# Holding x by features instead of by tokens through two transformer blocks, with each norm's root multiplied into the projections' results

## What is computed

```python
def rmsnorm(x, w):                       # norm_a, norm_c, final_norm; the second block's norms alike
    y = x * rsqrt(mean(x * x, axis=-1, keepdims=True) + EPS)
    return y * w
...
x = x + even_layer(rmsnorm(x, norm_a), w_in_a, ...)     # differential attention and a state-space scan
x = x + odd_layer(rmsnorm(x, norm_c), w_in_c, b_in_c, ...)   # sliding-window attention
x = rmsnorm(x, final_norm)
h = x + hybrid_mixer(rmsnorm(x, norm_mix), w_in, ...)   # stick breaking and two sparse attentions
h = h + memory_attention(h, mem, norm_mem_q, ...)
h = h + swiglu(rmsnorm(h, norm_ffn), w_ffn_in, w_ffn_out)   # (silu(a) * b) @ w_ffn_out, 2816 wide
return rmsnorm(h, norm_final)
```

## Time and profile before

| | us |
|---|---|
| median of 3 runs | 1584.45 (1584.28 to 1588.25) |
| the profiled execution, its own time | 1584.13 |
| its span | 1581.9 |
| PE busy in the span | 1534.0 (97%) |
| DVE, ACT, POOL busy | 820.4, 666.7, 260.6 |
| transfers | 150.20 MB, mean 95 GB/s |

### The profile page before, as it was taken

One profiled execution on the slowest core, in us unless ns is written; L12 is line 12 of the kernel. 1 busy time (PEld: TensorE's weight loads), 2 busy tenths in 40 slices (PEclk: granted clock), 3 DMA queues, 4 the chain that ended last, 5 costly groups with the idle time before them and its releaser, 6 DMA issues. The chain is left out here.

```text
span 1581.9 us, 20868 instructions
## 1 busy us (share of the span) xinstructions
PE 1534.0 (97%) x7886; PEld 1266.7 (80%) x7886; DVE 820.4 (52%) x1610; ACT 666.7 (42%) x1385; POOL 260.6 (16%) x166
## 2 busy tenths in 40 slices
PE   9999999999999999998999999899999999999998
PEld 7888878888787889877888777678866888888886
DVE  4322289858734566536634477847666333333224
ACT  4222366566424377524235554643245322232122
POOL 0000044265300012200012232313311000000000
PEclk9999999999999999999999999999999999999999
DMA  5226255311322431023521211213211222322322
GB/s 215 94 94 186 94 154 153 94 54 54 120 94 68 148 86 54 28 93 107 149 94 54 80 56 59 101 41 107 94 67 54 94 94 97 103 93 93 105 95 80
DMA packets 47458, 150.20 MB, mean 95 GB/s; under 512 B 6464, under 2 KB 6848, under 8 KB 47232
## 3 DMA queue, kind: packets, MB, share of 16 engines
q1 hardware_dynamic: 41664, 136.34, 26.8%
q10 hardware_dynamic: 5696, 12.55, 2.6%
HBM read 128.02 MB, written 2.10 MB: 82 GB/s over the span
## 5 line engine op out<-in xcount | busy, mean ns | idle before, releaser
L224 ACT ACTIVATE cut_hi<-raw 128x1024 fp32r<-128x1024 f32 x228 | 241.7, 1060 | 575.5 <-PE ps L241 571.2
L241 PE MATMUL ps<-h_hi,cut_hi 128*128 128x512 f32 (+1 forms) x1120 | 446.3, 399 | 5.5 <-DVE h_lo L449 2.8
L229 DVE TENSOR_TENSOR cut_lo<-raw,cut_hi 128x1024 fp32r<-128x1024 f32 x172 | 214.4, 1246 | 456.6 <-ACT cut_hi L224 454.9
L243 PE MATMUL ps<-h_hi,cut_lo 128*128 128x512 f32 (+1 forms) x1120 | 435.4, 389 | 0.0
L242 PE MATMUL ps<-h_lo,cut_hi 128*128 128x512 f32 (+1 forms) x1120 | 435.0, 388 | 0.0
L241 PEld LDWEIGHTS ps<-h_hi,cut_hi 128*128 128x128 f32 x1120 | 210.6, 188 | 56.2 <-issue 13.0
L243 PEld LDWEIGHTS ps<-h_hi,cut_lo 128*128 128x128 f32 x1120 | 210.4, 188 | 44.6
L242 PEld LDWEIGHTS ps<-h_lo,cut_hi 128*128 128x128 f32 x1120 | 210.9, 188 | 37.6
L229 POOL TENSOR_TENSOR cut_lo<-raw,cut_hi 128x1024 fp32r<-128x1024 f32 x56 | 135.4, 2418 | 467.4 <-ACT cut_hi L224 467.4
L241 PE MATMUL ps<-cut_hi,h_hi 128*128 128x512 f32 (+1 forms) x304 | 117.5, 387 | 3.3 <-DVE cut_lo L229 2.9
L243 PE MATMUL ps<-cut_hi,h_lo 128*128 128x512 f32 (+1 forms) x304 | 116.6, 384 | 0.0
(11 more groups left out here) (350 smaller groups left out, 2244.2 us busy)
## 6 DMA issues: line engine op xcount, KB each, us to landing
raw<-weights SPq DMA_DIRECT2D x228, 512.0 KB, 3.3
tiles_r<-tiles_r SPq DMA_DIRECT2D x96, 128.0 KB, 2.3
scr<-scr ACTq DMA_DIRECT2D x34, 64.0 KB, 3.6
x<-x_in SPq DMA_DIRECT2D x4, 512.0 KB, 6.1
x<-x_in ACTq DMA_DIRECT2D x1, 2048.0 KB, 8.8
q_stack<-qT_lo ACTq DMA_DIRECT2D x16, 128.0 KB, 2.3
out<-x SPq DMA_DIRECT2D x4, 512.0 KB, 2.6
consts<-tables ACTq DMA_DIRECT2D x1, 1732.0 KB, 8.0
```

Of the source, the lines that this page charges most:

```text
L224: act.activation(cut_hi[:, u % CUT, :], raw[:, u % RAW, :], ACT.Copy).then_inc(hi_ready, 1)
L229: eng.tensor_tensor(cut_lo[:, u % CUT, :], raw[:, u % RAW, :], cut_hi[:, u % CUT, :].bitcast(F32), ALU.subtract).then_inc(lo_ready, 1)
L241: a = pe.matmul(out, left[0], right[0], start=start, stop=False)
L243: return a, pe.matmul(out, left[1], right[0], start=False, stop=stop)
```

## The change

- The host turns x before and the output after the launch. In the kernel `xf` has eight tiles of 128 features x 512 tokens, so a product's bank can be added to it without a turn, and the weights stand on the left in `Combine`.
- A `Norm` no longer scales or turns anything. For each of the eight feature tiles ACT makes the high part of x times the gain and then the square, DVE the low part, and POOL adds up the eight squares. PE sums over the partitions with four one-column matmuls behind the first unit (`total`), DVE adds the epsilon, POOL takes the power, PE spreads the root over all partitions with four matmuls behind the sixth block of the second unit (`spread`), and ACT copies it into `root_row`. The results of the projections are multiplied by `root_row` on DVE.
- In `in_a` the first four units multiply the unscaled halves. The others multiply scaled ones, which DVE, ACT and POOL make meanwhile (`later`). In the mixer, plain results come first, and the cosine and sine rows are multiplied by the root ahead of the rotated ones; its two norms in one have totals and spreads twice.
- For `norm_c`, `norm_m`, `norm_q` and `norm_f` POOL cuts the first unit's low part, between its additions.
- Both query units now precede the memory attention. Its output weight is multiplied by halves of 256 tokens, and so are the last two units of the feed-forward part.
- The last norm works on features. The root is exp(-0.5 ln(mean + eps)) on ACT, once for each half of the tokens; there are eight stores of 256 KB instead of four of 512 KB.

```diff
         class Norm(Part):
...
-                    act.activation(self.xs[:, t, :], self.src[:, t, :], ACT.Square, scale=D ** -0.5,
-                                   accum_out=ss[:, t:t + 1])\
...
-                        last = pe.transpose(ps[:, k, t * P:(t + 1) * P], self.xs[:, t, k * P:(k + 1) * P], ident)
...
+            sum_bank, row_bank, at_s = 6, 7, 40
+            total_after, row_after = (0, KD - 1), (1, 5)
...
+            def high(self, act):
...
+                act.activation(self.to[0][:, k, :], xf[:, k, :], ACT.Copy, scale=col(self.gain, k)).then_inc(self.out_hi, 1)
+                if k >= 2:
+                    act.wait_ge(self.summed, max(k - 2, 1))
+                act.activation(self.square_at(k), xf[:, k, :], ACT.Square, scale=D ** -0.5).then_inc(self.squared, 1)
...
             def act(self, act):
...
+                while self.did_high < KD:
+                    if self.did_high == KD // 2 and not self.tables:
+                        cut_high(act, self.first)
+                    self.high(act)
...
+            def pool(self, pool):
+                for k in range(1, KD):
+                    if k == KD // 2 and not self.tables:
+                        cut_low(pool, self.first)
+                    self.add_square(pool, k)
+                self.root(pool)
+                if self.later:
+                    self.late_low(pool)
...
+            def beside_pe(self, pe, unit, k):
+                if (unit, k) == self.total_after:
+                    pe.wait_ge(self.summed, KD - 1)
+                    self.total(pe, total_row, 0)
+                if (unit, k) == self.row_after:
+                    pe.wait_ge(self.rooted, 1)
+                    self.spread(pe, self.row_bank, self.at_s)
...
         class MemoryAttention(Part):
...
+            def ready(self, k):
+                return self.out_dve, 4 + k // 2 + 1
...
         class FeedForward(Part):
...
                         cut_high(act, self.u0 + 2 * j + 1)
-                        act.wait_ge(self.done, 2 * j + 1)
-                        if j >= 3:
-                            act.wait_ge(self.prod, j - 2)
-                        act.activation(silu_of[:, j % 3, :], ps[:, 2 * j % 8, :], ACT.Silu).then_inc(self.silu, 1)
+                        if j == 0:
+                            norm_f.beside_act(act, 1)
                         cut_high(act, self.u0 + 2 * j + 2)
+                        act.wait_ge(self.rooted, j + 1)
+                        act.activation(silu_of[:, j % 3, :], silu_of[:, j % 3, :], ACT.Silu).then_inc(self.silu, 1)
...
+        class OutF(Combine):
...
+            def log_root(self, act, h):
+                act.wait_ge(self.totalled, 1 if h == 0 else 3)
+                act.activation(self.root(h), ps[:, 2 * h, 0:256], ACT.Ln, bias=eps_b).then_inc(self.logged, 1)
+                act.wait_ge(self.logged, h + 1)
+                act.activation(self.root(h), self.root(h), ACT.Exp, scale=-0.5).then_inc(self.rowed, 1)
...
+                for j in range(4):
+                    self.square(act, 1, j)
+                self.log_root(act, 0)
+                for k in (6, 7):
+                    self.weigh(act, 1, k)
+                self.log_root(act, 1)
```

More of the change, by code:

```diff
@@ new lines, in total, with spread @@
+            def total(self, pe, row, at):
+                for t in range(NT):
+                    last = pe.matmul(ps[:, self.sum_bank, at + t:at + t + 1], row[:, t * P:(t + 1) * P], one,
+                                     start=True, stop=True)
+                last.then_inc(self.totalled, 1)
+            def spread(self, pe, bank, a):
+                for t in range(NT):
+                    last = pe.matmul(ps[:, bank, t * P:(t + 1) * P], rs[:, a + t:a + t + 1].broadcast_to([P, P]),
+                                     ident, start=True, stop=True)
+                last.then_inc(self.rowed, 1)
@@ new lines, in beside_pe, with beside_act @@
+            def beside_pe(self, pe, unit, k):
[5 more added lines that the diff above has]
+                    self.spread(pe, self.row_bank, self.at_s)
+            def beside_act(self, act, f):
+                if f == 1:
+                    act.wait_ge(self.rowed, 1)
+                    act.activation(root_row, ps[:, self.row_bank, :], ACT.Copy).then_inc(self.row_out, 1)
+                if self.later and f in (2, 3):
+                    for k in range(4 * f - 8, 4 * f - 4):
+                        act.wait_ge(self.scaled, k + 1)
+                        act.activation(h_hi[:, k, :], self.later(k), ACT.Copy).then_inc(self.late_hi, 1)
@@ L487, in __init__ @@
                     self.starts += range(KD * j, KD * (j + 1), bk)
-                self.norm, self.low, self.beside = norm, low, beside
+                self.norm, self.low, self.beside, self.early = norm, low, beside, early
+                self.row_from = norm
                 self.widths, self.last_unit = [], []
+                self.biased = 0
+                if any(o[1] == "scaled bias" for o in outs):
+                    self.bias_chain = sem(tag + "_bias_chain")
                 u = 0
@@ L1910, in build @@
         stacks = Stacks()
-        in_c = Projection("in_c", "in_c", jobs, outs, banks=(0, 1, 2, 3, 4, 5, 0, 1, 4, 5), norm=norm_c, beside=stacks)
+        in_c = Projection("in_c", "in_c", jobs, outs, banks=(0, 1, 2, 3, 4, 5, 0, 1, 4, 5), norm=norm_c, beside=stacks,
+                          early=10)
         class KeyCopies(Part):
@@ L2309, in pe, with wait_swapped @@
+            def wait_swapped(self, eng, i):
+                slot = range(i % 4, i + 1, 4)
+                eng.wait_ge(swapped[i % 4], sum(self.rows(m) // 2 for m in slot))
             def pe(self, pe):
+                hi, lo = norm_m.to
                 for j in range(N_FT):
@@ L3294, in dve @@
                         cut_low(dve, self.u0 + 1)
-                    if step == self.n + 1:
-                        self.add(dve, 0)
-                for t in range(1, NT):
-                    self.add(dve, t)
+                for half in range(2):
+                    for pair in range(4):
+                        self.add(dve, half, pair)
+                        if half and pair:
+                            self.after.low(dve)
+                            self.after.low(dve)
         memory = MemoryAttention()
-        last_read[START["mem_out"] + 1] = fill_q.done, 1
-        norm_f = Norm("norm_f", x, NT, EPS_B, "norm_ffn", part(0, [NT, D]), memory.ready,
-                      first=START["ffn_in"], after=memory)
+        norm_f = Norm("norm_f", EPS_B, "norm_ffn", (h_hi, h_lo), memory.ready, START["ffn_in"], after=memory)
         ff = halves("ff", ARENA, ARENA + NFF * S, NFF)
@@ L3374, in tables @@
+        ffn_out = OutF("ffn_out", "ffn_out", lambda k: (ff[0][:, k, :], ff[1][:, k, :]), NFF, before=GatedUnits())
+        run(memory, norm_f, FeedForward(), ffn_out)
 def tables():
```

910 lines of the change are left out of this document (538 added, 372 removed).

## The result

The changed kernel takes **1632.16 us**, median of 4 runs (1630.08 to 1633.34), against 1586.35 for the kernel before beside it: ratio **1.0287**, 95% interval 1.0266 to 1.0308. It is slower, as forecast, but by 46 us and not by 13, and far outside the range (1580 to 1604). The profiled execution took 1632.14 us, its span is 1629.2 us at a mean granted clock of 0.984 (before 1581.9 at 0.995).

The account below looks back on a forecast made before the run. PE, busy 97% of the span, was taken to bound the kernel. Terms for start, norms, memory attention, end and smaller items summed to +13.25 us on the profiled 1584.13, giving 1597.4 us, range 1580 to 1604.

Parts of the forecast that it names:

- The end: Behind the last product: 13.3 us plus 0.8 on PE instead of 7.6, with three table loads uncovered; +6.5 (+4 to +8).
- the rival with fewer loads: At the end logarithm and exponential share a table, so two loads of 1.28 go: 1594.8 us, chance 0.03.
- The third feed-forward unit's wait: Behind `norm_f`, PE waits 1.7 us because the third unit's high part stands behind the copy of the root.
- The first gaps: At `norm_c` the first product comes 1.4 us behind the last; at the two norms in one POOL's low part 4.6 behind.
- The two rivals with closed gaps or covered waits: All norm gaps close to 1.4 + 2.0 (5.4 if doubled): 1577.7 us, chance 0.12; new waits are covered: 1586, chance 0.16.
- those rows show a slowing, not turns: Argument that POOL's 1.62 for 1.04 and DVE's 1.14 for 0.74 beside each other mean slowing, against a 1602.4 us sum.
- the rival's: At the start, `norm_f` and `norm_q`, DVE's low parts and POOL's additions take turns: +5, 1602.4 us, chance 0.20.
- At the start, where the sum had 0.9: First unit: transposes go, but POOL's seven additions delay the total; products begin at 17.9 against 17.0, +0.9 (-2.5 to +3).
- cost nothing: eight banks and PE's pace cover them: DVE's multiplications by the root and the feed-forward part's extra step add 0; uncovered, up to 2.3 us a pair.
- one more cut (1.2) behind the first gap: At the two norms in one the second unit's cut waits another 1.2 us; gap 9.8 instead of 10.5, -0.7.
- Late low parts ahead of the fifth unit: Fourth to fifth unit: scaled tiles pass DVE, ACT and POOL and may come late, +1.5 us (0 to +3.1).
- `norm_q` and memory attention: `norm_q` gap 4.9 instead of 5.7, -0.8; memory attention's first step uncovered, +2.3 (0 to +4.5); stage forecast +2.1.

Follow-up runs that it names:

- experiment 3: Changed kernel with the third feed-forward unit's high part ahead of the root's copy and one table load at the end instead of three: 1632.67 us.
- Experiment 5: Kernel before with unread series of DVE and POOL additions, alone and beside each other, behind its last norm: 1614.94 us in all, one execution.
- experiment 6: Changed kernel with POOL adding only 8 of 512 columns of the squares and totals taken over the last square: 1614.49 us.
- experiment 7: Changed kernel with the squares at all five norms added on DVE instead of POOL, everything computed: 1620.8 us.
- experiment 9: Changed kernel without the bias of the eight gates beside the sliding window, one DVE operation each instead of two: 1624.66 us.
- experiment 10: Kernel before with the sliding-window gates' bias added in a second DVE operation, eight times: 1588.23 us against 1585.98, ratio 1.0019.
- experiment 1: Changed kernel with the second unit's high and low parts ahead of the last squares and the seven additions, at the two norms in one: 1629.53 us.
- experiment 2: experiment 1 plus total and spread of the two norms in one moved one unit later: 1628.23 us.
- experiment 4: Changed kernel with unread matmuls filling PE's waits at the start and at three norms: 1631.92 us.

## Why the prediction was wrong where it was

**Right.** The direction, and the terms on the path that could be read from single rows. The end: 14.4 us from the last product for 13.3, with three loads of 1.28, so the rival with fewer loads fell; the six last multiplications took 3.57 where the sum had 2.4. The Trainium skill's drain ("ScalarE: Activation LUTs", What ACT_TABLE_LOAD costs) doesn't show: 0.01 us lies between activation and load, and 0.02 between load and next activation. The third feed-forward unit's wait: 1.7 for 1.7, removed by the order of ACT alone (experiment 3). Total and spread: 0.87 and 0.81 in `norm_f` for 0.9 and 1.1. The first gaps at `norm_c` (1.3 for 1.4) and at the two norms in one (4.3 for 4.6). `ffn_out` to the tenth. The two rivals with closed gaps or covered waits fell with the start, which is 9.1 longer, and with `norm_q` and `norm_f`, where the first product waits 3.75 and 7.43 for POOL's low part.

**Wrong, first step: "those rows show a slowing, not turns."** The likelier of two readings of 1.62 and 1.14 was the rival's. Experiment 5 shows turns. What POOL's additions cost, with turns, their own time and all that stands behind them, is 17.7 us (experiment 6); 11.4 of it comes back when DVE makes them all (experiment 7). The rival's own sum had 5. Two things made it larger than that sum: at the two norms in one DVE has additions too, fourteen in all with POOL's, and each delay passes to a cut that PE waits for. The price was low as well: the 1.04 of the earlier trace rows is another operation, and an addition of two tiles takes POOL 1.23 alone. At the start, where the sum had 0.9, 5.8 is left without the fifth unit's waits. About 1.0 of this is a misreading of the base: the second unit of the kernel before begins at 21.41, a unit of 5.44 behind 16.0 and not behind 17.0.

**Wrong, second step: the extra steps of DVE "cost nothing: eight banks and PE's pace cover them."** The cover was counted in DVE's time, and that did hold: 0.49 us fits. What it moved was the order in time of a two-element operation and POOL's cut, in the sliding window. Experiments 9 and 10 show it with and without the rest of the change: 4.3 to 4.4 us of waits, 3.0 net in the kernel before. The prediction looked for turns only where POOL got new work, and as a sign against this claim it named waits in the mixer and the feed-forward part, not here.

**Wrong, third step: the order of DVE at the two norms in one.** The prediction put one more cut (1.2) behind the first gap. The additions of the second norm, seven on DVE, stand ahead of that cut; the order could have been read before. 6.9 us of idle time; experiments 1 and 2 show that moving the cut alone passes the wait on to the next one.

**Missing: the clock.** No term of the sum had it. The profile after has a mean of 0.984 for 0.995. Executions of one kernel give an idea of what this is worth: those of experiment 1 take from 1624.61 us at 0.987 to 1631.3 at 0.981, those of the kernel before 1583.68 at 0.997 to 1587.08 at 0.993, so about 1 us for 0.001. From that 0.011 is some 11 us of the 46, an estimate and rather a high one: experiment 4 has 0.988 to 0.989 in three executions and is no faster. The two stages where nothing was edited show 6.1 directly, of which 0.35 is a longer wait (1.68 us at 357 for 1.33). It lies in the rows above, in part beside the other causes.

**Smaller.** Late low parts ahead of the fifth unit cost 3.3 for 1.5, a little above the given bound of 3.1. `norm_q` and memory attention together have 1.9 more than forecast, and their parts weren't tried one by one.

**Open.** Why one wait of 1.9 us is followed by a half clock and another of the same length, on the same instruction, isn't. At the start the kernel before and that of experiment 10 run the same instructions, and the granted clock from 13 to 16 us is 0.50 in one profile and 1.00 in the other. The Trainium skill ("TensorE: Matmul & The Clock Gate", What's actually happening) says that the gate's watch runs freely and doesn't start with the kernel; that would fit stretches that move with every edit, but no run here shows it.

## What to carry to other kernels

Before work goes to a second elementwise engine, ask whether DVE and POOL will both read two SBUF operands in the same stretch: if so, add their times, and one engine doing both can be faster. A new operation of half a microsecond is not free because its engine has room: see which short operation it pushes behind the start of a long one on the other engine, and who waits for that. And a change that adds waits to PE can pay again in granted clock (here an estimated 11 us at most; experiment 10 added 4.3 us of waits and paid nothing in clock), so leave room for that in the range.

## What the runs showed of the hardware beyond that

- An operation on 128 x 2 takes 0.15 us, and 1.2 to 2.35 beside a POOL operation: it waits for what is left of it, not for a share.
- A DVE operation with a single SBUF operand isn't free of it either: six `tensor_scalar` on 128 x 512 took 1.06 each beside POOL in experiment 5 (0.49 at L674 ahead of POOL's cut), and POOL's four took 5.46 instead of 4.92, while operations with one input in PSUM kept 0.61 and left POOL at 4.93.
- Filling PE's idle time with matmuls brought the full clock back right behind three of the five filled waits (1.00 at 14 to 22, 732 to 740 and 1194 to 1200 us) and none of the time (experiment 4).
